# Router inside the mixing layers' blocks by token tiles, and gate and up weights by quarters of the contraction

## The reference

```python
x = x + mix
h = rms_norm_2(x, norm_ffn_g[layer])
g_logits = hf @ w_group + b_group            # 4 groups
g_top = argmax(g_logits); g_w = softmax(g_logits)[rows, g_top]
e_logits = (hf @ w_expert + b_expert)        # 32 experts, those of the chosen group
top_p, top_j = top_k(softmax(e_logits), 2)
gates = g_w[:, None] * top_p / sum(top_p)
hidden = silu(xb @ w_gate[e]) * (xb @ w_up[e])
y = (hidden @ w_down[e]) * gate              # summed into the chosen tokens
x = x + y
```

## Time and profile before

| | |
|---|---|
| median of 3 runs | 1679.83 us (1677.62 to 1680.51) |
| profiled execution | 1681.06 us, span 1679.3 us |
| mean granted TensorE clock | 0.92 of full |
| TensorE busy (matmul) | 1379.4 us, 82% |
| VectorE, ScalarE, GpSimd busy | 385.7, 271.8, 96.1 us |
| DMA from memory | 494.05 MB, 295 GB/s over the span |

### The profile page before, as it was taken

The page is one execution under the profiler, slowest core; times in us unless marked ns, Lnnn a source line. Parts: engine busy times, 40 slices in busy tenths (PEclk is TensorE's granted clock), DMA queues, the critical chain, the costliest instruction groups (busy, mean ns, idle before and its releaser), DMA issues. The chain is left out here.

```text
span 1679.3 us, 21935 instructions
## 1 busy us (share of the span) xinstructions
PE 1379.4 (82%) x9400; PEld 752.2 (45%) x9400; DVE 385.7 (23%) x759; ACT 271.8 (16%) x518; POOL 96.1 (6%) x98
## 2 busy tenths in 40 slices
PE   7999999997999899677676767898998776767676
PEld 3755456544868464232232323555553322323232
DVE  2331232322545441011010100174321000001000
ACT  1131311322412111210000000114111110101110
POOL 0000000000000006294000000000000000000000
PEclk9999999998999999889788888899999887988988
DMA  9822543236330469999999999625459999999996
GB/s 370 286 78 107 194 150 125 101 125 217 132 119 4 191 242 426 428 429 428 428 429 428 428 429 427 287 103 197 157 232 427 429 429 428 428 429 429 428 429 286
DMA packets 41946, 497.01 MB, mean 296 GB/s; under 512 B 6432, under 2 KB 9248, under 8 KB 11552
## 3 DMA queue, kind: packets, MB, share of 16 engines
q1 hardware_dynamic: 41888, 496.17, 71.8%
HBM read 494.05 MB, written 2.10 MB: 295 GB/s over the span
## 5 line engine op out<-in xcount | busy, mean ns | idle before, releaser
L2456 PE MATMUL banks<-weight_ring,arena 128*32 128x512 f32 x1920 | 278.5, 733 | 199.2 <-DMA weight_ring<-in_moe_weights 197.6
L2456 PEld LDWEIGHTS banks<-weight_ring,arena 128*32 128x32 f32 x1920 | 75.9, 131 | 396.1 <-issue 394.2
L2417 DVE TENSOR_TENSOR arena<-arena,banks 64x512 f32<-64x512 f32 x32 | 22.1, 690 | 675.4 <-ACT arena L2375 675.4
L813 PE MATMUL banks<-weight_ring,hT 128*128 128x512 f32 x384 | 169.1, 597 | 1.5 <-DMA weight_ring<-in_ring_weights 1.5
L2444 PEld LDWEIGHTS banks<-arena,x_normed 128*128 128x128 f32 x1088 | 124.0, 192 | 30.2 <-issue 28.6
L2467 PE MATMUL banks<-weight_ring,arena 128*32 128x512 f32 x1024 | 131.7, 660 | 0.0
L2444 PE MATMUL banks<-arena,x_normed 128*128 128x64 f32 x1088 | 128.7, 276 | 1.3 <-DVE arena L2403 1.3
L321 PE MATMUL banks<-weight_ring,hT 128*128 128x512 f32 x256 | 112.8, 596 | 0.0
L813 PEld LDWEIGHTS banks<-weight_ring,hT 128*128 128x128 f32 x384 | 72.8, 192 | 87.7 <-issue 85.6
L2375 ACT ACTIVATE arena<-banks 64x512 f32<-64x512 f32 x32 | 18.9, 591 | 531.1 <-PE banks L2456 531.1
L2495 PE MATMUL banks<-arena 64*128 64x512 f32 x256 | 63.6, 611 | 25.6 <-ACT arena L2381 25.6
(11 more groups left out here) (482 smaller groups left out, 1384.9 us busy)
## 6 DMA issues: line engine op xcount, KB each, us to landing
weight_ring<-in_moe_weights SPq DMA_DIRECT2D x184, 2048.0 KB, 20.5
weight_ring<-in_ring_weights SPq DMA_DIRECT2D x36, 2048.0 KB, 8.8
arena<-in_moe_weights SPq DMA_DIRECT2D x4, 2048.0 KB, 10.0
weight_ring<-in_ring_weights SPq DMA_DIRECT2D x4, 1024.0 KB, 5.2
mix<-in_moe_weights SPq DMA_DIRECT2D x2, 2048.0 KB, 13.6
hT<-in_moe_weights SPq DMA_DIRECT2D x2, 1024.0 KB, 5.3
arena<-in_moe_weights SPq DMA_DIRECT2D x2, 1024.0 KB, 7.4
arena<-in_c_even SPq DMA_DIRECT2D x1, 1440.0 KB, 6.4
```

What stands on the lines that cost most here:

```text
L813: ins = pe.matmul(bank, g.hT[:, k, half * P:(half + 1) * P], w[:, k, :], start=(k == 0), stop=(k == KT - 1))
L2417: dve.tensor_tensor(hid[0:2 * CAP, :], sil[0:2 * CAP, :], b_gu[2 * CAP:4 * CAP, :], ALU.mult).then_inc(s_h, 1)
L2456: ins = pe.matmul(b_gu[q:q + CAP, :], xg[:, 4 * half + k, e * CAP:(e + 1) * CAP], up_w(where, 2 * half + e, which)[:, k, :], start=(half = ...
```

## The change

1. The router's block is gone. A class `Router` issues its work within the mixing layer's block, by token tile: the output pieces come in the order tile 0 (two halves of the width), tile 1, and square sums, roots, transposes and logits of tile 0 go between the last pieces.
2. Logits come from unscaled x: x itself is transposed (into `xT`, arena 0 to 2047) and multiplied by router weights that carry the gain (`wg`), and the logits are scaled by the reciprocal root when VectorE takes them. The scaled x (`xs`) is still made, for the gather.
3. The selection has fewer steps (constants `order`, `slots`, `full` in place of additions and comparisons), the gates are made behind the ranks, and 48 `keep_clock` matmuls become 16.
4. Gate and up weights lie by quarters of the contraction in slots 0 to 3, each with both experts. TensorE waits for one slot at a time, and each slot is released and reloaded on its own.
5. On SP's queue: the fourth extra slot is loaded behind the second, slot 4 one output piece later, `odd_par` last, when the logits are done (the `xT` place is part of its target).

Cut to its core:

```diff
@@ even_layer, sync
             sp.dma_start(moe_params(g), A["moe_par"][0]).then_inc(g.moe_par_landed[0], 16)
-            sp.dma_start(g.odd_par, A["odd_par"]).then_inc(g.odd_par_landed, 16)
             weights(1, 0, extra[0][0], second)
             weights(1, 1, extra[1][0], second)
-            sp.wait_ge(s_w, 2)
+            router.fourth(sp)
+            sp.wait_ge(s_w, 3)
             weights(0, 4, ring[4], first)
             sp.wait_ge(s_w, 4)
             weights(0, 5, ring[5], first)
             weights(1, 2, extra[2][0], second)
+            sp.wait_ge(router.s_lg, TT)
+            sp.dma_start(g.odd_par, A["odd_par"]).then_inc(g.odd_par_landed, 16)
@@ even_layer, scalar (odd_layer alike)
+            y_out(0)
+            y_root(0)
+            y_out(1)
+            mix_copy(0)
+            y_root(1)
+            mix_copy(1)
+            router.squares(act, 0, 0)
+            router.squares(act, 0, 1)
+            router.root(act, 0)
+            router.copy_x(act, 0, 0)
+            router.copy_x(act, 0, 1)
+            router.squares(act, 1, 0)
+            router.copy_x(act, 1, 0)
+            router.squares(act, 1, 1)
+            router.root(act, 1)
+            router.copy_x(act, 1, 1)
+            router.exps(act)
@@ even_layer and odd_layer, vector
+            router.prepare(dve)
             for j in range(4):
-                ch, tt = divmod(j, 2)
+                tt, ch = divmod(j, 2)
                 w = g.x[:, tt, ch * 512:(ch + 1) * 512]
                 dve.wait_ge(s_w, j + 1)
                 TT_(w, w, ps[j], ALU.add).then_inc(s_add, 1)
-            dve.wait_ge(s_add, 4)
+                if j == 0:
+                    router.scale_weights(dve)
+                    router.eps(dve, 0)
+                if j == 1:
+                    router.inverse(dve, 0)
+                    router.scale_x(dve, 0)
+                if j == 2:
+                    router.eps(dve, 1)
+            router.logits_out(dve, 0)
+            router.inverse(dve, 1)
+            router.logits_out(dve, 1)
+            router.select(dve)
+            router.gates(dve)
@@ even_layer, tensor
+            out_part(0, (4, 5, 6, 7))
+            out_part(1, (4, 5, 6, 7))
+            out_part(2, (4, 5, 6, 7))
+            mix_transposes(0)
+            out_part(3, (4, 5, 6, 7))
+            pe.wait_ge(s_mT, 1)
+            out_part(0, (0, 1, 2, 3)).then_inc(s_w, 1)
+            mix_transposes(1)
+            out_part(1, (0, 1, 2, 3)).then_inc(s_w, 1)
             pe.wait_ge(s_mT, 2)
-            for j in range(4):
-                out_part(j, (0, 1, 2, 3)).then_inc(s_w, 1)
-    g.end_phase()
+            out_part(2, (0, 1, 2, 3)).then_inc(s_w, 1)
+            router.x_transposes(pe, 0, 0)
+            router.x_transposes(pe, 0, 1)
+            out_part(3, (0, 1, 2, 3)).then_inc(s_w, 1)
+            router.x_transposes(pe, 1, 0)
+            router.logits(pe, 0)
+            router.x_transposes(pe, 1, 1)
+            router.logits(pe, 1)
+            router.ranks(pe)
+    g.end_phase(router.sems)
@@ Router
+    def logits_out(self, dve, tt):
+        dve.wait_ge(self.s_lg, tt + 1)
+        dve.scalar_tensor_tensor(out=self.lg[:, tt, :], in0=self.g.ps[4 + tt][:, 0:36], scalar=self.rstd[:, tt:tt + 1],
+                                 in1=self.brow, op0=ALU.mult, op1=ALU.add).then_inc(self.s_lo, 1)
...
+        dve.tensor_tensor(sel, oh1, oh2, ALU.add).then_inc(self.s_sel, 1)
+        dve.tensor_tensor(c2(318), c2(306), c2(304), ALU.subtract).then_inc(self.s_gd, 1)
+        self.scale_x(dve, 1)
+        dve.wait_ge(self.s_ex, 2)
...
+    def ranks(self, pe):
+        g, ps, sel = self.g, self.g.ps, self.sel
+        pe.wait_ge(self.s_zero, 2)
+        pe.wait_ge(self.s_x, 4)
+        for b in range(4):
+            ins = pe.matmul(ps[b][:, :], self.zeros[:, 0:P], self.zeros, start=True, stop=False)
+        ins.then_inc(self.s_Pt, 1)
+        pe.wait_ge(self.s_xT, 4)
+        self.keep_clock(pe, 6)
+        pe.wait_ge(self.s_lo, TT)
+        pe.wait_ge(self.s_sel, 1)
...
+        self.keep_clock(pe, 10)
@@ moe_layer, sync
-            released = (s_ga, s_ga, s_gu, s_gu, s_da, s_dn)
+            def released(j, n, more):
+                sp.wait_ge(*((s_gu, n * 4 + (more * 4 + j - 3)) if j < 4 else ((s_da, s_dn)[j - 4], n + more)))
...
             for j in range(4, 6):
-                sp.wait_ge(s_ga, 1)
+                released(j - 4, 0, 1)
                 load(1, 1, j)
...
             if c0 < g.limit:
-                sp.wait_ge(s_ga, T * NP)
-                g.send(sp, c0 + 2)
-                sp.wait_ge(s_gu, T * NP)
-                g.send(sp, c0 + 4)
...
+                for j in range(SLOTS):
+                    sp.wait_ge(*((s_gu, T * NP * 4) if j < 4 else ((s_da, s_dn)[j - 4], T * NP)))
+                    g.send(sp, c0 + j + 1)
@@ moe_layer, tensor
-            def gate_up(half, group, m):
+            def gate_up(quarter, group, m):
                 where = at_pair[group]
-                for e in range(2):
-                    pe.wait_ge(landed[group][2 * half + e], 16 * len(where[2 * half + e]) * (m + 1))
-                for k in range(4):
+                pe.wait_ge(landed[group][quarter], 16 * len(where[quarter]) * (m + 1))
+                for k in range(2):
...
+                ins.then_inc(s_gu, 1)
```

More of the change, by code:

```diff
@@ L2351, in _ @@
                         for j in range(SLOTS):
[L2352 removed]
+                            released(j, t * NP, pair + NP)
                             load(2, pair, j)
@@ L2473, in of_pair @@
                 pe.wait_ge(s_xg, n + 1)
-                gate_up(0, group, m).then_inc(s_ga, 1)
-                gate_up(1, group, m).then_inc(s_gu, 1)
+                for quarter in range(4):
+                    gate_up(quarter, group, m)
                 gather(n + 1)
```

449 lines of the change are left out of this document (251 added, 198 removed).

## The result

The changed kernel takes **1664.2 us** (median of 5 runs, 1661.56 to 1669.19) against 1679.83 (the median of 5 runs too): a ratio of 0.991 with an interval of 0.9895 to 0.9933, so 15.6 us faster, where 25.3 were forecast. The direction was right; the time lies 9.7 us above the forecast and just outside its range (1664.0).

A forecast was written before the change was run, and what follows sets the result against it. Expert loops were taken as bound by DMA, the rest by chains of waits ahead of them. Even side 9.9 - 1.3 + 0.3 + 2.5 = 11.4, odd 11.1 + 0.3 + 2.5 = 13.9, together 25.3 us: 1654.5 us, range 1647 to 1664.

The forecast's parts named there:

- What bounds the kernel: Whole kernel: expert loops are a fixed amount of transfer, 411 us each; the rest is chains of waits ahead of them.
- TensorE is 9.9 us earlier: Ahead of the first loop (even layer): the interleaved router lets gather and gate/up start 9.9 us sooner.
- 11.1: Ahead of the second loop (odd layer): the same walk starts gate/up 11.1 us earlier, with nothing late loaded.
- rival (a): Router and loop ends: clocks kinder than taken, selection then limits; 1649.4 us, chance 0.17.
- that sign of being wrong: End of the router: the forecast is wrong if selection instead of TensorE ends it.
- Minus 1.3 us: Ahead of the first loop: the odd layer's parameters land late, VectorE sends x out 1.3 us later; bounds 0 and 3.
- the quarter's gain of 1.77 us: Start of a loop: with quarters the first ring load leaves 1.77 us sooner.
- Net 0.3 us a loop: Start of a loop: first load 1.77 us earlier, less a 1.5 us hole behind the sixth load; bounds 0 and 1.8.
- Rival (b): Router's interleaved stretch: waits drop narrow matmuls to 1.2 GHz, 11 us lost; 1665.5 us, chance 0.12.
- 2.5 us a loop: End of a loop: only a quarter follows the last landing, winning 2.5 us, the middle between clock cases.
- (c): Expert loops: quarters with gaps hold the clock low, TensorE falls behind DMA; 1727 us, chance 0.03.
- (d): Ahead of the loops: the earlier TensorE meets a DMA backlog, losing 9.5 us of gain; 1664 us, chance 0.03.

The follow-up runs named there:

- Experiment 1: Changed kernel with the odd layer's parameters issued one load earlier on SP's queue, ahead of the third extra slot: 1658.78 us, ratio 0.990.
- experiment 7: Changed kernel with pair 1's gather issued twice in both loops, its first copy overwritten: 1667.28 us, ratio 0.994.
- Experiment 9: Changed kernel with 10 clock-keeping records ahead of the first gather and, behind it, 48 in the first loop, 4 in the second: 1659.51 us, ratio 0.988.
- the wide ring: Changed kernel with pair 2's down weights in two extra slots: second loop only 1660.18 us; both loops, with the odd layer's parameters one load earlier, 1651.11 us.
- experiment 2: Changed kernel with gate and up weights waited for and released by halves, the layout by quarters kept: 1668.99 us, ratio 0.994.
- experiments 10: Changed kernel with parameters earlier, pair 2's down weights in extra slots (both loops), 10 clock-keeping records ahead of the first gather, 4 behind: 1652.78 us, ratio 0.984.
- 11: Changed kernel with parameters one load earlier and clock-keeping records ahead of the first gather (10) and behind it (4), ring unchanged: 1654.18 us, ratio 0.987.
- experiment 12: Kernel of 11 with 16 more clock-keeping records ahead of every quarter from the fourth pair on: 1652.62 us, ratio 0.986.

## Why the prediction was right or wrong

**What bounds the kernel: right.** What the change won or lost lies in the first ring loads, the length of the streams and the tails; the steady stretch stays at 428 to 429 GB/s. TensorE waits for landings by quarters as foretold, though not four times some 3 us: the four waits of the last pair are 0.2, 3.0, 1.7 and 3.0 us.

**"TensorE is 9.9 us earlier" (even), 11.1 (odd): the router's walk was too cautious, its exit was left out.** To the clock keeping behind the ranks (593.04, 1209.15) the changed kernel gained 12.3 and 12.1 us, against 10.0 and about 11 worked out. Part of it is the kinder clock of rival (a): the sum-opening matmuls took 3.7 us in the even layer instead of 5.2 (in the odd one 5.4 as before). In the even layer the selection ended the router, if only by 0.35 us (TensorE's wait ahead of the ranks at 591.93), where the forecast had TensorE; that sign of being wrong came true there and cost next to nothing. But from there to the gather it takes 4.1 and 3.9 us instead of 3.1, 1.0 and 0.8 us a layer that no term had: TensorE stands idle for 1.4 to 1.6 us where 0.65 stood. A block ended there before too, but without `end_phase`, which now stands there; that this is the reason is likely and not tested. In sum the gather starts 11.3 us earlier in both layers.

**"Minus 1.3 us", bounds 0 and 3: the first failed step.** From gather to gate/up the change takes 10.15 us instead of 4.57, 5.6 us lost. Counted from the anchor, the bulk of the bytes was there when the forecast had it (602.0 - 552.88 = 49.1, for 604.4 - 555.15 = 49.25). But the step took 428 GB/s up to the last byte, and the last packets came at 37 GB/s: the load landed 2.1 us later than worked out (51.34 behind the anchor), with VectorE right behind it. Its piece and the way out of x took 0.7 us more than taken, and the gather ended 1.4 us sooner (48.0 behind the anchor for 49.45), so that much more of the lateness showed: 1.3 + 2.1 + 0.7 + 1.4 = 5.5. Beyond that, TensorE's clock was at half behind this wait of 6.4 us, and with it the quarter's gain of 1.77 us at the first ring load was gone (3.70 us after the start of gate/up, as before). Experiment 1 gives 6.8 us back in its trace. Where a load lands behind a chain that is being shortened, each microsecond won upstream is one lost there, and the bounds of 0 and 3 had no room for that.

**"Net 0.3 us a loop": the second failed step, and the larger.** The mechanism was foretold, down to the place (behind the sixth load, gated by pair 1's first down half) and, at full clock, to the size: 1.5 forecast, 1.2 to 1.6 us in the narrow-ring loops without slow spells. (The first bytes move 0.96 us after an issue in the trace of before, where the step took 1.75; as this stands on both sides of the comparison it changes little.) What was missing is that this hole grows one for one with any delay of TensorE between the first ring load and pair 1's first half of down: +3.5 us for a doubled gather of 3.6 (experiment 7), +3.2 us for slow downs (seventh load 34.1 us after the first instead of 30.8). The step took TensorE's full clock in pairs 0 and 1. Rival (b) had the low clock in the narrow stretch of the router; it came in the pairs behind it. The second loop's first load also lost 1.3 us to a slow gather and 1.65 to a slow first quarter. Experiment 9, in whose trace those pairs ran at full clock, gives 10.8 us back; the wide ring gets most of the streams' share without it.

**"2.5 us a loop" at the end: right** (2.45 and 2.6 us; experiment 2 takes it back). It was a middle between two ends, and neither end happened: the last quarters took 3.21 and 3.45 us after waits of about 2 and 3 us, near the 3.54 of the low clock, but the gather behind them ran at full clock. That was luck in part: experiments 10 and 11 have tails of 25 us, longer than the 21.4 of before, which the bounds didn't allow. The prediction weighed a rule of the Trainium skill (TensorE: Matmul & The Clock Gate, section "HAM oscillation — how this bites in real kernels"): short groups behind waits for their weights start at the low clock. It is mostly borne out: in the eleven traces with waits for single quarters and no records in them, 264 of the 304 quarters behind waits of 2.9 to 3.05 us took 2.4 to 3.64 us, and 40 took 1.92.

**The range** failed by treating the sizes as independent. A late load counts once: in experiment 1 the first ring load left 6.8 us sooner and the stream stayed at 423.9 us. But the low clock, which none of the terms for the loops' starts had, counts at every place where a load waits for TensorE: at the first ring load (gather and first quarter) and again in the hole (the downs). Rivals (c) and (d) didn't happen: experiment 12 shows that even with TensorE 90% busy the loop stays DMA's.

**Open:** why downs of pairs 0 and 1 are slow in some executions: in 12 of the 24 loops traced with the router inside the blocks (4 of the 8 with records ahead of the gather), in none of the 4 loops with the old router, which are too few to blame the new one. The instructions right ahead of them, with their waits of 0.55 us, are the same in all.

## What to carry to other kernels

When a loop is bound by transfers, the work ahead of it is worth something only up to the point where the first load waits for a release that the saving doesn't move; find that load and ask what delays its releaser, clock included. When a chain is shortened, list every load whose landing is set by the transfers and not by the chain, and set it against the new times, not the old; reckon with a slow last piece of the load. A few cheap matmuls in the known waits (1.2 us here) held the clock of gather and gate/up, but not of the downs 12 us later; a slot that comes free earlier made the clock matter less.

## What the runs showed of the hardware

- Waits of 1.4 to 1.6 us ahead of the first gather, after a stretch of narrow matmuls, were followed by a slow gather (4.9 to 6.3 us instead of 3.79) in 10 of 16 loops, and by a slow gate/up (8.45 to 10.0 us instead of 7.07) in 12; in the two loops where gate/up alone was slow, TensorE had waited 6.4 and 6.2 us ahead of it. A longer wait wasn't the worse one: the gather was slow behind all 7 waits of 1.43 to 1.46 us and behind 3 of the 9 of 1.58 to 1.61. With 10 records in that wait and 4 (once 48) behind the gather both ran at full clock in 8 of 8.
- The last packets of a 1390 KB load behind a full queue came at 37 GB/s for 1.8 us after 416 GB/s before; its landing stood 0.4 us behind them, and the first instruction that waited for it started 0.03 us later.
- Equal waits of 2.9 to 3.05 us left TensorE at either level within one trace: 264 of 304 quarters behind them took 2.4 to 3.64 us, the others 1.92. Behind waits of over 5.5 us all 47 halves (before and experiment 2) took 5.0 to 6.6 us instead of 3.64. With the waits filled all quarters took 1.92 (experiment 12).
- A loop's tail of some 19 us (last landing to the next layer) was 25.0 us in two of the traces, with the whole difference in the clock: last quarter 3.64 for 1.92, gather 7.09 for 3.79, and the rest in down and the small matmuls ahead of it.
